# Forgetting attention on one core: high and low parts stacked in the matmul operands, a second buffer for the exponentials, projections in the order query, key, value, and another order of work around the softmax chain

## What is computed

```python
kvf = rmsnorm(h, kv_norm) @ w_kvf                 # keys, values, forget logits
log_f = jax.nn.log_sigmoid(f_logit)
cum_log_f = jnp.cumsum(log_f, axis=1).transpose(0, 2, 1)
...
q = (hn @ wq) * (HEAD_DIM ** -0.5)
s = jnp.einsum('bhqd,bhkd->bhqk', qb, k).astype(jnp.float32)
s = s + fq[..., None] - cum_log_f[:, :, None, :]
s = jnp.where(mask[None, None], s, -jnp.inf)
p = jax.nn.softmax(s, axis=-1)
o = jnp.einsum('bhqk,bhkd->bhqd', p.astype(v.dtype), v)
...
return o @ wo
```

## Time and profile before

| | |
|---|---|
| median of 3 runs | 2467.12 us (2464.04 to 2469.94) |
| profiled execution | 2473.14 us, span 2471.4 us |
| PE busy | 2340.3 us (95%) |
| DVE, ACT, POOL busy | 57%, 36%, 8% |
| matmuls | 10838 |
| the stage of the change in this execution | about 632 to 884 us |

### The profile page before, as it was taken

One profiled execution on the slowest core, in us unless ns is written; L12 is line 12 of the kernel. 1 busy time (PEld: TensorE's weight loads), 2 busy tenths in 40 slices (PEclk: granted clock), 3 DMA queues, 4 the chain that ended last, 5 costly groups with the idle time before them and its releaser, 6 DMA issues.

```text
span 2471.4 us, 30025 instructions
## 1 busy us (share of the span) xinstructions
PE 2340.3 (95%) x10838; PEld 1938.3 (78%) x10838; DVE 1405.0 (57%) x1986; ACT 880.9 (36%) x1316; POOL 203.2 (8%) x154
## 2 busy tenths in 40 slices
PE   2779999999899999999999999999999899999999
PEld 2677788888788877888877778878888688888887
DVE  6855554456666665454447657773445547654443
ACT  3213332223445533222245435553434443322221
POOL 5502200002100030000020000002000001200000
PEclk7959999999999999999999989999999999999999
DMA  2352232222211112222222211213223212232222
GB/s 114 50 131 84 94 102 94 95 100 94 71 55 58 61 60 94 95 101 94 97 82 78 85 60 54 67 61 109 94 102 128 68 60 94 96 101 94 98 98 85
DMA packets 77174, 213.72 MB, mean 86 GB/s; under 512 B 18320, under 2 KB 26768, under 8 KB 76688
## 3 DMA queue, kind: packets, MB, share of 16 engines
q1 hardware_dynamic: 70880, 205.14, 25.6%
q10 hardware_dynamic: 6192, 7.19, 0.9%
HBM read 203.78 MB, written 4.19 MB: 84 GB/s over the span
## 4 chain that ended last, share of the span: by engine, by line
PE 83%; DVE 6%; ACT 4%; POOL 2%; DMA 2%; issue 2%; SPq 1%; ACTq 0%; DVEq 0%; POOLq 0%
PE lin L423 25%; PE lin L424 25%; PE lin L425 25%; ACT w_hi L811 1%; DVE w_lo L1179 1%; SPq L337 1%; PE tr L690 1%; POOL ssm_cl L1772 1%; PE tr L584 1%; POOL tmp_c L1771 1%; POOL ssm_cl L1770 1%; DMA cols<-cols 1%; DMA ssm_mt<-ssm_kp 1%; DVE fox_pl L1471 1%; PE tr L736 0%
## 5 line engine op out<-in xcount | busy, mean ns | idle before, releaser
L811 ACT ACTIVATE w_hi<-w_raw 128x1024 fp32r<-128x1024 f32 x369 | 390.8, 1059 | 1067.2 <-PE lin L425 1063.7
L423 PE MATMUL lin<-x_hi,w_hi 128*128 128x512 f32 x1472 | 594.8, 404 | 4.4 <-DVE w_lo L1179 2.6
L424 PE MATMUL lin<-x_lo,w_hi 128*128 128x512 f32 x1472 | 575.7, 391 | 0.0
L425 PE MATMUL lin<-x_hi,w_lo 128*128 128x512 f32 x1472 | 575.7, 391 | 0.0
L1179 DVE TENSOR_TENSOR w_lo<-w_raw,w_hi 128x1024 fp32r<-128x1024 f32 x369 | 468.7, 1270 | 110.3 <-ACT w_hi L811 109.6
L423 PEld LDWEIGHTS lin<-x_hi,w_hi 128*128 128x128 f32 x1472 | 278.5, 189 | 72.2 <-issue 9.5
L424 PEld LDWEIGHTS lin<-x_lo,w_hi 128*128 128x128 f32 x1472 | 278.4, 189 | 65.5 <-issue 9.5
L425 PEld LDWEIGHTS lin<-x_hi,w_lo 128*128 128x128 f32 x1472 | 277.8, 189 | 58.8
L423 PE MATMUL lin<-q_hi,w_hi 128*128 128x512 f32 x688 | 271.5, 395 | 7.9 <-DVE q_lo L1184 6.0
L424 PE MATMUL lin<-q_lo,w_hi 128*128 128x512 f32 x688 | 270.7, 394 | 0.0
L425 PE MATMUL lin<-q_hi,w_lo 128*128 128x512 f32 x688 | 270.4, 393 | 0.0
(11 more groups left out here) (405 smaller groups left out, 2858.3 us busy)
## 6 DMA issues: line engine op xcount, KB each, us to landing
w_raw<-w SPq DMA_DIRECT2D x369, 512.0 KB, 3.3
ssm_mt<-ssm_kp SPq DMA_DIRECT2D x64, 64.0 KB, 2.8
ssm_u<-x_a SPq DMA_DIRECT2D x1, 2048.0 KB, 12.2
resid<-x_b ACTq DMA_DIRECT2D x1, 2048.0 KB, 10.6
z_b<-z_scratch SPq DMA_DIRECT2D x4, 512.0 KB, 4.6
out<-resid SPq DMA_DIRECT2D x8, 256.0 KB, 2.1
z_scratch<-ssm_y SPq DMA_DIRECT2D x16, 64.0 KB, 2.3
z_scratch<-ssm_y ACTq DMA_DIRECT2D x16, 64.0 KB, 2.6
```

The costliest lines, as they stand in the source:

```text
L423: nc.tensor.matmul(out, WH[:, b, w], xh[:, k, 0:cols], start=(k == 0), stop=False)
L424: nc.tensor.matmul(out, WH[:, b, w], xl[:, k, 0:cols], start=False, stop=False)
L425: last = nc.tensor.matmul(out, WL[:, b, w], xh[:, k, 0:cols], start=False, stop=(k == KC - 1))
L811: nc.scalar.activation(WH[:, b, :], raw[:, r, :], ACT.Copy).then_inc(s_hi, 1)
```

## The change

**Scores.** The query and key tiles are laid out anew. fox_qa holds the high queries in the head's half and the low queries in the other half; fox_ka the high keys in both halves; fox_qb the high queries and the forget rows; fox_kb the low keys and the forget rows. The product a x a gives high x high plus low x high, b x b gives high x low plus the forget terms: two products for three. ScalarE writes two more copies for queries and two more for keys per pair (semaphore s_dup), VectorE writes the low queries into the other half.

**Values.** fox_v holds for each key block and head 64 high columns and 64 low columns side by side. One product with fox_ph gives high x high in PSUM rows 0 to 63 and low x high in rows 64 to 127; one product of 64 columns adds high x fox_pl: two products for three. ScalarE copies rows 64 to 127 out (`fox_fold`), VectorE adds (`fox_sum`) and ScalarE and VectorE split the sum (`fox_out`), where both read PSUM before.

**Order.** The slabs of a pair come as queries, keys, values. fox_e has two buffers, and the scores of the second head go ahead of the first head's transposes. The first head's value products stand in the middle of the second linear (behind chunk 5 of 8), and need all three high parts but only the first low part; their low products wait for the rest. In the beginning of the stage the gates are finished first, and the forget rows of both heads are issued ahead of the first query copies.

The diff, cut:

```diff
-            def causal_scores(qh, ql, kh, kl, rows):
+            def causal_scores(par):
...
-                    nc.tensor.matmul(out, qh[rows, q], kh[rows, 0:n], start=True, stop=False)
-                    nc.tensor.matmul(out, qh[rows, q], kl[rows, 0:n], start=False, stop=False)
-                    nc.tensor.matmul(out, ql[rows, q], kh[rows, 0:n], start=False, stop=False)
+                    nc.tensor.matmul(out, FQA[:, par, q], FKA[:, par, 0:n], start=True, stop=False)
+                    nc.tensor.matmul(out, FQB[:, par, q], FKB[:, par, 0:n], start=False, stop=False)
...
-            def probs_out(pair):
...
+            def probs_out(pair, par):
...
+                def product(kb, low):
+                    _, _, o = prob_place(kb)
+                    n, v = slice(o, o + L - kb * P), FV[:, pair % 2, kb, par, :]
+                    if low:
+                        return nc.tensor.matmul(out[0:HD, kb * P:L], v[:, 0:HD], F_PL[:, n], start=False, stop=False)
+                    return nc.tensor.matmul(out[:, kb * P:L], v, F_PH[:, n], start=(kb == 0), stop=(kb == TB - 1))
+                pe.wait_ge(s_ph, c.up(s_ph, 3))
                 pe.wait_ge(s_pl, c.up(s_pl))
-                causal_values(TR[0], FVH[:, pair % 2], FVL[:, pair % 2], F_PH, F_PL, slice(0, P))
+                for kb in range(TB - 1):
+                    product(kb, False)
+                pe.wait_ge(s_pl, c.up(s_pl, 2))
+                for kb in range(TB):
+                    product(kb, True)
+                product(TB - 1, False).then_inc(s_o, 1)
...
-            linear(qkv[0], AH, AL)
-            linear(qkv[1], XH, XL)
+            linear(qkv[0], XH, XL)
+            linear(qkv[1], AH, AL)
             linear(qkv[2], AH, AL)
             fox_scores(0)
-            pe.wait_ge(s_evac, qkv[0].done())
+            pe.wait_ge(s_evac, qkv[2].done())
             values_turn()
             for pair in range(HEADS // 2):
                 more = pair + 1 < HEADS // 2
                 nxt = qkv[3 * pair + 3:3 * pair + 6]
                 if more:
-                    linear(nxt[0], AH, AL)
+                    linear(nxt[0], XH, XL)
                 else:
                     fox_o_part(early[0], range(KC - 1))
-                pe.wait_ge(s_x, X0 + 2 * pair)
-                pe.wait_ge(s_vt, pair + 1)
-                causal_transposes(F_E)
                 pe.wait_ge(s_e, c.up(s_e, TB))
                 fox_scores(2 * pair + 1)
-                probs_out(pair)
+                pe.wait_ge(s_sum, 2 * pair)
+                pe.wait_ge(s_vt, pair + 1)
+                causal_transposes(F_E[0])
                 if more:
-                    linear(nxt[1], XH, XL)
+                    linear(nxt[1], AH, AL, mid=lambda: probs_out(pair, 0), mid_at=5)
                 else:
-                    fox_o_part(early[1], range(KC - 1))
-                pe.wait_ge(s_x, X0 + 2 * pair + 1)
-                causal_transposes(F_E)
+                    fox_o_part(early[1], range(5))
+                    probs_out(pair, 0)
+                    fox_o_part(early[1], range(5, KC - 1))
+                pe.wait_ge(s_sum, 2 * pair + 1)
+                causal_transposes(F_E[1])
                 if more:
                     linear(nxt[2], AH, AL)
-                probs_out(pair)
+                probs_out(pair, 1)
                 pe.wait_ge(s_e, c.up(s_e, TB))
                 if more:
-                    pe.wait_ge(s_evac, nxt[0].done())
+                    fox_scores(2 * pair + 2)
+                    pe.wait_ge(s_evac, nxt[2].done())
                     values_turn()
-                    fox_scores(2 * pair + 2)
...
-            def fox_hi(j, dst):
+            def fox_q_hi(j):
...
-                    hi(dst[HALF[par], par, :], T[HALF[par], :])
-            split_hi(fox_slab(0))
+                    hi(FQB[HALF[par], par, :], T[HALF[par], :])
+                    nc.scalar.activation(FQA[HALF[par], par, :], T[HALF[par], :], ACT.Copy).then_inc(s_dup, 1)
...
+            def fox_k_hi(j):
...
+                    hi(FKA[HALF[par], par, :], T[HALF[par], :])
+                    nc.scalar.activation(FKA[HALF[1 - par], par, :], T[HALF[par], :], ACT.Copy).then_inc(s_dup, 1)
...
+            split_hi(fox_slab(0))
             act.wait_ge(s_pad, 1)
-            split_hi(fox_slab(1))
-            fox_hi(1, FQH)
             act.wait_ge(s_rows, 1)
...
-            forget_rows(0)
+            for par in range(2):
+                forget_rows(par)
...
+            def fox_fold(par):
+                act.wait_ge(s_o, c.up(s_o))
+                nc.scalar.activation(FOLD[par][0:HD, :], TR[0][HD:P, :], ACT.Copy).then_inc(s_fold, 1)
...
             def fox_out(par, ch):
-                rows = slice(HD * par, HD * par + HD)
-                act.wait_ge(s_o, c.up(s_o))
-                nc.scalar.activation(row(QH[rows], ch), TR[0][rows, :], ACT.Copy).then_inc(s_oh, 1)
+                act.wait_ge(s_sum, 2 * ch + par + 1)
+                nc.scalar.activation(QH[HALF[par], ch, :], ACC[HALF[par], :], ACT.Copy).then_inc(s_oh, 1)
...
-            fox_hi(2, FKH)
+                hi(FV[:, par].rearrange("p b h e -> p (b h) e")[:, :, 0:HD], TR[1][:].rearrange("p (n d) -> p n d", d=HD))
+            fox_q_hi(0)
+            split_hi(fox_slab(1))
+            fox_k_hi(1)
             split_hi(fox_slab(2))
-            forget_rows(1)
-            causal_exps(F_E)
+            causal_exps(F_E[0])
...
+                causal_exps(F_E[1])
                 causal_hi(F_PH)
-                causal_exps(F_E)
+                fox_fold(0)
+                if more:
+                    fox_q_hi(j)
+                    split_hi(fox_slab(j + 1))
+                causal_hi(F_PH)
+                if more:
+                    fox_k_hi(j + 1)
                 fox_out(0, pair)
                 if more:
-                    split_hi(fox_slab(j + 1))
-                    fox_hi(j + 1, FQH)
-                causal_hi(F_PH)
-                if more:
-                    fox_hi(j + 2, FKH)
                     split_hi(fox_slab(j + 2))
+                fox_fold(1)
                 fox_out(1, pair)
                 if more:
-                    causal_exps(F_E)
+                    causal_exps(F_E[0])
                     fox_v_hi((pair + 1) % 2)
...
                 for par in range(2):
-                    lo(l[HALF[par], par, :], T[HALF[par], :], h[HALF[par], par, :], s_qk)
-                split_lo(sl)
+                    lo(FQA[HALF[1 - par], par, :], T[HALF[par], :], FQB[HALF[par], par, :], s_qk)
+                c.up(s_dup, 2)
+            def fox_k_lo():
+                for par in range(2):
...
+                    TT(l[:, s], TR[bank][:, 0:n], f32(h[:, s]), ALU.subtract).then_inc(s_pl, 1)
...
+            def fox_sum(par):
+                dve.wait_ge(s_fold, c.up(s_fold))
+                dve.wait_ge(s_x, c.now(s_x))
+                TT(ACC[HALF[par], :], TR[0][0:HD, :], FOLD[par][0:HD, :], ALU.add).then_inc(s_sum, 1)
...
-                fox_probs()
+                fox_probs(F_E[0])
                 if more:
-                    fox_value(j)
+                    fox_evac(j, HD ** -0.5)
+                causal_max()
+                if more:
+                    fox_weights(j)
                 causal_lo(F_PH, F_PL)
-                causal_max()
-                fox_out(0, pair)
-                fox_probs()
+                fox_probs(F_E[1])
+                fox_sum(0)
                 if more:
-                    fox_split(j + 1, HD ** -0.5, FQH, FQL)
+                    fox_q_lo()
+                    fox_evac(j + 1, 1.0)
+                    fox_weights(j + 1)
                 causal_lo(F_PH, F_PL)
                 if more:
-                    fox_split(j + 2, 1.0, FKH, FKL)
+                    fox_k_lo()
+                fox_out(0, pair)
+                if more:
+                    fox_value(j + 2)
+                fox_sum(1)
+                if more:
+                    causal_max()
                 fox_out(1, pair)
                 if more:
-                    causal_max()
                     fox_v_lo((pair + 1) % 2)
```

78 lines of the change are left out of this document (46 added, 32 removed).

## The result

The changed kernel takes **2442.64 us** (median of four runs, 2440.8 to 2444.1), the kernel before 2468.53 beside it: ratio 0.9896, with a 95% interval of 0.9883 to 0.9909, a gain of 25.9 us (22.5 to 28.9). Three further comparisons of the same kernel gave 0.9891, 0.9889 and 0.9912.

What follows compares the result with a forecast made beforehand. TensorE's queue and stalls were taken to bound the kernel. Seven pairs -20.8, head +4.0 and tail -1.2 give -18.0 us: 2473.14 profiled becomes 2455.1, less 6.0 for the median 2449.1 us, range 2444 to 2457.

Steps and rivals of the forecast that it cites:

- The cut products: In each pair on TensorE, four sets of score and value matmuls fewer at 0.62 each: 2.48 us gained.
- The wait: In each pair, TensorE's stall of 0.60 us before the first head's value products goes, covered by 1.1 us.
- a restart of the cut linear: In each pair, cutting the second linear in two costs TensorE 0.1 us (0 to 0.3).
- The turned values: The four transposes of the values in each pair, read as 0.56 us on TensorE; no change booked.
- rival (1): Forget rows come late in every pair, long chain 0.4 to 1.1 us over its slack: 2454 us; chance 0.15.
- The head: Start of the stage: third linear starts after 10.5 us of idle TensorE; 4.0 us lost (3.3 to 7).
- The tail: From the last pair to the output projection's last slice: 1.2 us gained (0 to 2.5).
- (2): Head costs 3 to 4 us more, clock staying low through third linear, second DMA batch delaying more: 2453; chance 0.08.
- (4): Steps across partition halves cost more: twice the price 2457 us, chance 0.04; four times 2474, chance 0.03.
- (5): The cut matmuls don't shorten TensorE's queue; no time given; chance 0.02.
- (3): TensorE gains 3 to 5 us more, 64-column low value products having shorter weight loads, head at lower bound: 2445; chance 0.08.
- The held start: On VectorE, half-tile steps can't overlap across partition groups: 0.09 each, seven per pair, 0.6 us more; long chain 0.1 to 0.2.

Runs made afterwards that it cites:

- the second profile of the kernel before: The kernel before run once more with no edit, for a second profile: 2468.59 us.
- The two experiments on the head: Changed kernel with high queries ahead of row issues (2442.62, 2442.51, 2436.96); the same plus third slab's w_lo and query evacuation moved into VectorE's gate waits (2432.96, 2432.05).
- the second pair of profiles: Both kernels run again with no edit: changed kernel 2442.17 us (ratio 0.9891), kernel before 2468.59 us.

## Why the prediction was right or wrong, point by point

**The cut products: nearly right.** A set was priced at 0.62 by the value products; measured 0.64 and 0.66. 4 x 0.62 = 2.48 against 2.59: 0.8 us over seven pairs.

**The wait: the step that failed.** The mechanism was right, the wait goes, but the sum priced it at 0.60, the idle time of one row, less 0.10 for a restart of the cut linear, 0.50 in all. Taking that wait away alone is worth 0.83, the cut included. The rows that would have told it were in the trace of the kernel before: the scores ahead of the wait take 3.15, and 2.39 where none follows, and the value products behind it are 0.11 slower. 0.33 a pair, 2.3 us. The restart, for which no row of before had a price, was nearly right (0.07 for 0.1); what was missing is the refund at the old place, 0.16 booked as busy and 0.11 behind the wait.

**The turned values: left out.** The prediction has them at 0.56 before and after; moved behind the scores they take 0.37. 1.4 us over seven pairs. It read the 0.56 as work, and for rival (1) it read the scores at 687.16 as starting without a wait; by the rows 0.18 of it is most likely the wait for the low keys. So it would be the same kind of slip as the one above: a wait taken from the idle column, which here showed none.
Together 0.8 + 2.3 + 1.4 = 4.5, for the 4.4 by which the pairs were off.

**The head: right in its steps, and in its sum partly by luck.** The third linear was put at `f_s` + 16.35 (655.1 - 638.75), and it started there (650.28 - 633.93). Idle 10.71 for 10.5 (the prediction's own marks, 655.1 less 649.83 - 5.56, give 10.8), and the eight issues hold ScalarE for 5.1 of the 8.28 that its row calls issue. From the third linear to the first pair it is 9.92 for 9.9, but of two wrong parts: the work is 7.6 (5.56 + 1.66 + 0.37) and not 7.9, and the clock costs 2.3 and not 2.0. No row fixed this 2.0, it was a choice between 1.35 and 5.56. Against the second profile of the kernel before, the head loses 3.4. The two experiments on the head confirm the order of causes: the third linear waits for `w_lo`, that for the queries, those for the eight issues.

**The tail: too small.** -2.1 for -1.2 (-1.7 in the second pair of profiles). The wait ahead of the value products fell from 2.34 to 1.50, 0.84 and not 0.6, and the wait of some 0.2 for the sum ahead of the transposes didn't come; the 2.88 at the last slice is what was worked out (2.9).

**The rivals.** (1) The forget rows did not come late: the sync queue issues the last at about 680.7 (second of the two in the row below) and it lands 1.9 later by the median, 682.6, ahead of the scores at 683.07; slack 0.4 for 0.3. (2) The clock did not stay low through the third linear: it was granted at 0.50 for the first 5.0 us (650.28 to 655.28) and at 1.00 from there to the first pair, and the scores behind the linear start without a wait. (4) Steps across the halves cost the same as steps within one: the fold 0.60 across and 0.59 for the like within, the key copies 0.63 both ways, the low queries 0.69 across and 0.70 within, the sums 0.69 across (684.47) and 0.68 within. (5) The cut matmuls did shorten the queue, to the full. (3), "TensorE gains more", is the way it went, but not by its mechanism: the four low products with 64 columns take 0.58 for 1280 columns of stream (672.49 to 673.07), the three high ones 0.52 for 1152, the same 0.45 ns per column. These rows of the changed kernel show what (1) and (4) rest on, on the sync queue, ScalarE and VectorE:

```profile
680.10 1.22 SPq L386 DMA_DIRECT2D fox_kb<-f_rows  x2
```

```profile
673.37 0.60 ACT L1042 ACTIVATE sq<-tr 64x512 f32<-64x512 f32 x1 [2.58 <-PE tr L626]
...
674.39 0.62 ACT L999 ACTIVATE fox_qa<-t 64x512 fp32r<-64x512 f32 x1
```

```profile
674.00 0.68 DVE L1536 TENSOR_TENSOR acc<-tr,sq 64x512 f32<-64x512 f32 x1 [0.93 <-ACT sq L1042]
674.72 0.69 DVE L1217 SCALAR_TENSOR_TENSOR fox_qa<-t,fox_qb 64x512 fp32r<-64x512 f32 x1
```

**The rest.** The stage is 23.2 to 23.7 us shorter, the four comparisons average 0.9897, 25.4 us. The 2 us between are inside the interval of each comparison, and the stretches outside the stage scatter by more than that between executions; that they are nothing else, no run shows. The lowest distance of the pairs that the prediction allowed was 25.4, which it also named as a sign of being right; the 24.97 lie outside, and with them the time below the range. The way the kernel took is the one that was forecast all the same: no wait ahead of the value products in the pairs, no late forget row, and the same step that holds up the third linear.

The held start that the prediction weighed does show in these rows: the low query that follows the sum starts 0.04 behind its end (674.72, 674.68), not 0.09 ahead of it, and it cost nothing there. The 0.6 that the prediction worked out for VectorE from seven of them would be idle and not busy time, so the 20.88 can neither show nor deny it.

## What to carry over

Price a wait by the distance of two starts, with and without it, and not by the idle column: here 0.60 of idle were 0.83 us, and another 0.66 showed as 0.20. The waits of under 0.2 show in no idle column at all: look for a block that starts a little behind the end of what it reads, later than the pace of its engine has it. And a step that was off the critical path can come onto it at the head of a stage while it stays hidden in the loop: there, ask what each queue has in front of the one instruction that the bottleneck waits for.

## What was not expected of the hardware

- What DMA issues cost ScalarE depended on what stood in front of them. Ahead of the high queries eight issues held it for 5.1 us (641.31 to 646.40); behind them four issues (642.99 to 645.52) ran beside the four activations of the queries, and ScalarE was idle for 0.43.
- The stretch ahead of `f_s`, some 635 us of the same work in every kernel here, differed by 6.1 us between the 18 profiled executions (632.9 to 639.0), and none of it arose behind the first 300 us: from there on the distances between two traces stay the same to 0.05.
- After 10.71 us of idle TensorE the third linear and the scores behind it ran at a mean clock of 0.75, 0.50 (1.2 GHz) for 5.0 us and 1.00 behind it; behind waits of 1.2 us it stayed at 1.00.
